# A gated-delta solve with a forget attention between its levels, and the state's steps behind it: three queues reordered

## What is computed, cut to what matters

```python
sol = lax.linalg.triangular_solve(a_mat, rhs, left_side=True, lower=True)
u, w = sol[..., :dv], sol[..., dv:]
def step(state, xs):
    v_new = u_n - jnp.einsum("bhck,bhkv->bhcv", w_n, state)
    o = (jnp.einsum("bhck,bhkv->bhcv", q_n * jnp.exp(g_n)[..., None], state)
         + jnp.einsum("bhce,bhev->bhcv", attn_n, v_new))
    state = state * jnp.exp(gl_n)[..., None, None] + jnp.einsum("bhck,bhcv->bhkv", kt_n, v_new)
    return state, o
```

## Time and profile before

| what | value |
|---|---|
| median of 3 runs | 1621.25 us |
| the profiled execution's own time | 1622.98 us |
| its span in the profile | 1621.0 us |
| TensorE matmul busy | 82% of the span |
| VectorE busy / ScalarE busy | 38% / 30% |
| mean DMA rate | 320 GB/s |
| mean granted TensorE clock | 0.949 |

### The profile page before, as it was taken

One profiled execution on the slowest core, in us unless ns is written; L12 is line 12 of the kernel. 1 busy time (PEld: TensorE's weight loads), 2 busy tenths in 40 slices (PEclk: granted clock), 3 DMA queues, 4 the chain that ended last, 5 costly groups with the idle time before them and its releaser, 6 DMA issues.

```text
span 1621.0 us, 32850 instructions
## 1 busy us (share of the span) xinstructions
PE 1327.2 (82%) x14418; PEld 1048.5 (65%) x14418; DVE 608.0 (38%) x980; ACT 484.0 (30%) x811; POOL 0.2 (0%) x4
## 2 busy tenths in 40 slices
PE   9999999999999999998876586576676667558666
PEld 9999899999999999995543343343343344334333
DVE  7967556787986778641110010010110110011001
ACT  6846467556644554530000000000000000000001
POOL 0000000000000000000000000000000000000000
PEclk9999999999999999999998898898899898899889
DMA  8442034443656655799999999999999999999997
GB/s 333 160 152 98 35 134 151 173 171 132 219 207 263 252 177 193 263 343 424 429 428 429 431 428 429 431 429 427 435 429 427 429 429 433 426 429 431 428 433 310
DMA packets 42264, 517.92 MB, mean 320 GB/s; under 512 B 4816, under 2 KB 4944, under 8 KB 7248
## 3 DMA queue, kind: packets, MB, share of 16 engines
q1 hardware_dynamic: 42048, 516.71, 78.1%
q10 hardware_dynamic: 144, 0.17, 0.0%
HBM read 515.81 MB, written 1.05 MB: 319 GB/s over the span
## 4 chain that ended last, share of the span: by engine, by line
PE 50%; DMA 42%; DVE 4%; ACT 2%; issue 1%; SPq 1%; another core or an unknown queue 0%; DVEq 0%; ACTq 0%
DMA e_gu<-experts 42%; PE psum L346 11%; PE psum L347 11%; PE psum L348 11%; PE psum L986 7%; PE psum L1030 3%; DVE w_low L1696 1%; PE psum L602 1%; PE psum L1036 1%; DVE a_gdn_qk L1745 1%; DMA w_raw<-dense 0%; PE psum L962 0%; PE psum L1016 0%; SPq L2405 0%; PE psum L587 0%
## 5 line engine op out<-in xcount | busy, mean ns | idle before, releaser
L986 PE MATMUL psum<-e_gu,x_xt 128*32 128x256 f32 x3072 | 217.9, 447 | 175.2 <-DMA e_gu<-experts 175.1
L986 PEld LDWEIGHTS psum<-e_gu,x_xt 128*32 128x32 f32 x3072 | 108.3, 128 | 277.0 <-DMA e_gu<-experts 186.9
L346 PE MATMUL psum<-h_high,w_high 128*128 128x256 f32 x864 | 245.4, 284 | 0.6 <-DVE w_low L1696 0.6
L347 PE MATMUL psum<-h_low,w_high 128*128 128x256 f32 x864 | 242.7, 281 | 0.0
L348 PE MATMUL psum<-h_high,w_low 128*128 128x256 f32 x864 | 242.6, 281 | 0.0
L1696 DVE TENSOR_TENSOR w_low<-w_raw,w_high 128x2048 fp32r<-128x2048 f32 x99 | 225.7, 2288 | 28.0 <-ACT w_high L1119 20.6
L1119 ACT ACTIVATE w_high<-w_raw 128x2048 fp32r<-128x2048 f32 x99 | 189.2, 1914 | 60.2 <-PE psum L348 50.3
L2371 DVE COPY x_yb<-psum 128x256 f32<-128x256 f32 x64 | 27.2, 424 | 423.0 <-PE psum L1030 423.0
L346 PEld LDWEIGHTS psum<-h_high,w_high 128*128 128x128 f32 x864 | 162.8, 188 | 7.1 <-issue 4.7
L347 PEld LDWEIGHTS psum<-h_low,w_high 128*128 128x128 f32 x864 | 162.8, 188 | 0.1
L348 PEld LDWEIGHTS psum<-h_high,w_low 128*128 128x128 f32 x864 | 162.8, 188 | 0.0
(11 more groups left out here) (464 smaller groups left out, 2114.6 us busy)
## 6 DMA issues: line engine op xcount, KB each, us to landing
e_gu<-experts SPq DMA_DIRECT2D x44, 4096.0 KB, 52.9
w_raw<-dense SPq DMA_DIRECT2D x100, 1024.0 KB, 4.8
e_dn<-experts SPq DMA_DIRECT2D x45, 2048.0 KB, 49.4
e_dn<-experts SPq DMA_DIRECT2D x37, 1024.0 KB, 54.8
e_gu_lo<-experts SPq DMA_DIRECT2D x16, 2048.0 KB, 51.5
e_gu_hi<-experts SPq DMA_DIRECT2D x15, 2048.0 KB, 55.9
e_gu<-experts SPq DMA_DIRECT2D x8, 1024.0 KB, 6.4
e_gu<-experts SPq DMA_DIRECT2D x2, 1536.0 KB, 8.0
```

The lines of the kernel that those rows point to most:

```text
L346: mm(ps, w[0], src[0], start=start, stop=False, **kw)
L347: mm(ps, w[0], src[1], start=False, stop=False, **kw)
L986: last = mm(half(psum[32 * s:32 * s + 32, GU_BANK[j % 2], 0:256], P), X["xt"][:, k, CAP * j:CAP * (j + 1)], expert_gu(j, k)[:, :, s * P:(s ...
```

## The change

One wait is added to `state_d`; an empty entry goes into each of the three lists of the solve (behind `fox_turn(2)` on TensorE, behind the third head's exponentials on ScalarE, ahead of `fnorm(3)` on VectorE), so that everything behind it comes one slot later. Behind the solve, `state_d(0)` and `state_o(0)` change places on TensorE, and `state(0)` goes ahead of `sb_keep(0)` on VectorE.

```diff
             def state_d(n):
                 t, po = n // 2, CHUNK * (n % 2)
                 ps = aux.fill(pe, f"dS{n}")
+                pe.wait_ge(sem("gdn_vnew"), n + 1)
                 for hd in range(H):
...
-                            lambda: fox_scores(3), lambda: fox_turn(2),
+                            lambda: fox_scores(3), lambda: fox_turn(2), lambda: None,
                             lambda: (fox_turn(3), pv("fpv", 2, "fox_pT", A["pt"], A["fox_v"])),
...
             branch("a", ya, "ya", [
-                lambda: (state_o(0), sb_scores(0)), lambda: (state_d(0), sb_scores(1)), lambda: state_v(1),
+                lambda: (state_d(0), sb_scores(0)), lambda: (state_o(0), sb_scores(1)), lambda: state_v(1),
...
-                          lambda: softmax_exp(A["s"], A["st"], "fox", 2, FSP),
+                          lambda: softmax_exp(A["s"], A["st"], "fox", 2, FSP), lambda: None,
                           lambda: softmax_exp(A["s"], A["st"], "fox", 3, FSP),
...
-                          lambda: (fout(1), fmax(2)), lambda: (fnorm(2), fmax(3)), lambda: fnorm(3), lambda: fout(2),
+                          lambda: (fout(1), fmax(2)), lambda: (fnorm(2), fmax(3)), lambda: None, lambda: fnorm(3), lambda: fout(2),
...
-            sb_keep(0); state(0); lows("ga10"); lows("ga11"); sb_keep(1); mix("a", 0, 0); vnew(1); mix("a", 0, 1); sb_masked(0)
+            state(0); sb_keep(0); lows("ga10"); lows("ga11"); sb_keep(1); mix("a", 0, 0); vnew(1); mix("a", 0, 1); sb_masked(0)
```

## The result

The changed kernel took 1625.11 us (median of 13 runs, 1623.02 to 1625.99) against 1621.58 us for the kernel before in the same runs (13, 1620.27 to 1623.35): ratio 1.0022, 95% interval 1.0015 to 1.003. The forecast was 1622.4 us, with a range up to 1624.7; the result lies above it. The profiled execution took 1624.96 us, with a span of 1623.1 us where before it was 1621.0 us.

A forecast was written before the change was run, and what follows sets the result against it. TensorE was taken to bound the kernel up to some 750 us, full DMA behind it. On the profiled 1622.98 us, -3.4 (solve) and +2.8 (wait at output 1) gave -0.6: 1622.4 us, range 1619.4 to 1624.7.

The forecast's parts named there:

- The slots: Solve's fourth level: 1.9 us of idle TensorE and 1.8 us of low clock gained, 0.3 us charged; sum -3.4 us.
- The second part: Behind the solve, state before output: ScalarE waits for output 0, shifts 5.7 us, and TensorE loses 2.8 us at output 1.
- the sums' wait: TensorE at the sums of head 1: the shifted sb_keep(1) ends at 220.7, sums wanted at 220.53; 0.2 us.
- the bank of sz0: Bank output 1 takes, released by sb_masked(0) on VectorE: free at 224.2, wanted at 221.4.
- The transfer to the end: Expert stretch: loads are released by TensorE's progress, so gains or losses near 200 us move the end in full.
- the new wait: TensorE ahead of output 1: 2.8 us for a bank, the sums' 0.2 us included; bounds 0 to 3.3 us.
- the clock behind the new wait: Rival at output 1: clock falls after 2.8 us of idle, price 1.8 us, total 1624.2 us; chance 0.31.
- The forecast from the median: Whole kernel, if the median run had no clock dip in the solve: 1621.25 - 1.6 + 2.8 = 1622.5 us.

The follow-up runs named there:

- the run with the filler: Changed kernel with 11 products of constants on TensorE between the sums of head 1 and output 1: 1622.40 us against 1621.16 for the kernel before.
- the second part alone: Kernel before with only state ahead of output (TensorE and VectorE) and the added wait, solve as before: 1626.44 us against 1621.16.
- the first part: Kernel before with only the three empty entries in the solve's lists: 1619.34 us against 1621.16.
- the run with the early release: Changed kernel with vnew(1) and sb_masked(0) ahead of two mix on VectorE: 1620.62 us against 1621.64 for the kernel before.
- short filler: Changed kernel with 4 products of constants on TensorE ahead of output 1: 1624.46 us against 1621.64 for the kernel before.

## Why the prediction was wrong

**What held.** The slots: -3.4 us was the sum for the profiled execution, and -3.2 us was measured at the last level; the first U product was put at 182.7 and came at 182.78. The second part: ScalarE was to stand 5.6 us and stood 5.63; the sums' wait was put at 0.2 us; the bank of sz0 was named as what ends last, and the wait ahead of output 1 was 2.25 us between matmuls (0.2 and 2.5 us lost by the marks, 2.8 predicted together). Nothing else came late up to the expert stage. The transfer to the end was taken as complete; between the first two profiles it looks like 80% (2.1 of 2.67 us), but over the 13 profiles the end follows increment 1 with a slope of 1.00 (standard error 0.07), so complete is right. The rest of the sum can be checked by itself: the run with the filler has the solve's gain and the new wait, but no low clock, and it took 1622.40 us where the sum gave 1622.4 (the groups of runs differ by up to 0.5 us, so the last tenths of this agreement are luck). Two counts were wrong without effect: between 200.70 and 213.79 us ScalarE has five table loads and not four, and the added wait occurs three times and not four.

**What failed: the clock behind the new wait.** The sum was -3.4 + 2.8, with nothing in it for the clock behind the 2.8 us; I made that a rival, at chance 0.31 and a price of 1.8 us. The fall came in every profile with this wait, and in two of three it cost 3.1 us. Both the chance and the price were too low:

- Price: 1.8 us came from one low stretch of 3.4 us. Such a stretch costs 1.6 us where it can be compared: the last level's first U product starts at 186.02 with it and at 184.38 without, in two executions of the kernel before. Here the low stretch was nearly 7 us in two profiles (the whole change and the second part alone) and 3.4 us in a third. The filler run puts 3.1 us on the long one. The forecast's sum with that price is 1622.4 + 3.1 = 1625.5, and with the short one 1624.0; the median of the runs, 1625.11, lies between. Nothing in the trace of the kernel before foretold the long one for a wait of this length: behind its 13 waits of 3.18 to 3.20 us every low stretch lasted 3.4 us, and longer ones came only with waits of over 9 us.
- Chance: all three profiles with the full wait show a fall. Of the 13 runs 12 lie above 1624.4, and the filler's highest was 1623.04, so probably only the lowest run, 1623.02, can be one without a fall; this is an inference, for those runs have no profile. I had drawn the odds from two gaps in the expert stretch, one with a fall and one without. The same trace has 13 such waits of 3.18 to 3.20 us, and the clock was low behind 9 of them. Counting all would have made the fall the likelier case.

**What was right by luck, and what was right with reason.** The forecast from the median (1621.25 - 1.6 + 2.8) used the guess that the typical execution of the kernel before has no fall in the solve. Three of four profiles with that wait speak for it, and in them the last level's first U product (184.30 to 184.40) is 1.5 to 1.6 us later than in the changed kernel, the 1.6 us that the prediction had put for this case. It explains why the first part gives 1.8 us in the medians and 3.1 us between the two profiles, and why the whole change costs 3.5 us in the medians and 2.0 us between the profiles: against an execution without the fall, increment 1 moves from 227.53 to 231.91 us with the long low stretch, which is 4.4 us, and to 230.36 us with the short one, which is 2.8 us.

## What to carry to other kernels

When work is reordered on one engine, follow each value that moves later into the in-order list of its reader: here the state came over 7 us earlier to no one's gain, while a 0.4 us copy at the head of ScalarE's list held back over 12 us of table loads, logarithms and gates, and through them a bank. Price a new wait of TensorE with the clock behind it, from all comparable waits of a trace and from several executions. The fall can cost more than the wait (3.1 against 2.5 us here). A cheap filler over the whole wait took it away in the profile, and a release a few instructions earlier took it away in most runs, as far as the medians tell; a filler over part of the wait did not, in the profile or, by the median, in most runs. Run the parts of a change apart: one of these was worth keeping.

## What the hardware showed that I had not expected

The low clock does not have to follow its gap at once. In the second execution of the changed kernel it began 2.7 us after the wait had ended, in the run with the early release 2.9 us after a wait of only 0.44 us, with TensorE busy between. It lasted 3.4 us or nearly 7 us, with equal code and an equal wait of 2.25 us. A wait of 1.97 us in the solve was followed by a fall in one of four executions, a wait of 2.25 us behind the solve in three of three, and a wait of 1.36 us behind a short filler in the one profile there is, though that was the fastest of its runs. All five profiles with a wait at output 1, the one of 0.44 us too, have a low stretch behind it; the eight without one (the filler's among them) have full clock from 180 to 330 us. That the wait of 0.44 us caused its fall is not shown. The Trainium skill (TensorE: Matmul & The Clock Gate, section What's actually happening) says that the clock's monitor runs freely against the program; these executions agree with that. What decides between the short and the long low stretch is open, and so is how often each occurs in the unprofiled runs. The price of the long one is measured: 3.1 us, where the wait itself was 2.5 us.
